# Moving weight sums, head transposes, convolution passes and the next part's input inside a hand-ordered decoder-layer kernel

## The reference, cut to what matters

```
u = rmsnorm(x) @ w_in                         # 1024 -> q, k, v, gates, o, B, C, h
h = sigmoid(o) * HeadRMSNorm(mLSTM(q, k, v, gates))       # 4 heads, chunkwise with running state
y = B * causal_depthwise_conv3(C * h_conv)                # 3 taps, 512 channels
x = x + concat(h, y) @ w_out
x = x + (silu(f @ w_gate) * (f @ w_up)) @ w_down          # f = rmsnorm(x), D_FF = 2816
x = x + sigmoid(x @ w_pg) * rmsnorm(p @ w_ple)
y = rmsnorm(x)
```

## Time and profile before

| | |
|---|---|
| median of three runs | 2736.15 us |
| the profiled execution's own time | 2736.39 us |
| its span, first to last instruction | 2734.7 us |
| TensorE busy (matmul) | 2522.9 us, 92% |
| VectorE, ScalarE, GpSimd busy | 54%, 35%, 42% |
| mean granted TensorE clock | 0.966 of full |
| DMA | 456.46 MB, 167 GB/s on average |
| weight conversions, ScalarE and GpSimd | 696 each |
| sums stored in part 0, loaded later | 168 stores, 336 loads of 512 KB |

### The profile page before, as it was taken

How to read it: one execution, slowest core, us unless ns; L and a number is a source line. 1 busy time by engine, 2 the same in 40 slices (tenths; PEclk the granted TensorE clock), 3 DMA queues, 4 the chain that set the end, 5 groups by cost and what they waited for, 6 DMA issues and landing times.

```text
span 2734.7 us, 41185 instructions
## 1 busy us (share of the span) xinstructions
PE 2522.9 (92%) x15882; PEld 2458.5 (90%) x15882; DVE 1479.8 (54%) x2288; ACT 952.8 (35%) x1766; POOL 1138.3 (42%) x939
## 2 busy tenths in 40 slices
PE   4999788999999779999999999998998999999998
PEld 4889787999999778899999999997888989999997
DVE  5656787765546664447753333466455674333355
ACT  4344443333333534334422222253223442222233
POOL 3556655665555443333332333333422333233333
PEclk6999899999999989999999999998999999999998
DMA  5435534554444646456455545474545645554544
GB/s 163 168 139 199 178 116 147 177 188 160 169 168 149 201 141 198 141 182 202 154 178 166 152 149 162 150 232 151 178 141 178 198 159 175 186 163 153 161 142 161
DMA packets 306309, 456.46 MB, mean 167 GB/s; under 512 B 21683, under 2 KB 218596, under 8 KB 305606
## 3 DMA queue, kind: packets, MB, share of 16 engines
q1 hardware_dynamic: 239014, 269.13, 29.8%
q10 hardware_dynamic: 67104, 184.70, 21.4%
HBM read 347.44 MB, written 106.35 MB: 166 GB/s over the span
## 4 chain that ended last, share of the span: by engine, by line
PE 47%; DVE 4%; issue 2%; DMA 2%; ACT 1%; POOL 1%; DVEq 0%; POOLq 0%; SPq 0%; ACTq 0%
PE bank L503 15%; PE bank L504 15%; PE bank L505 15%; DMA wring<-weight_parts 1%; DVE ess L2130 0%; POOL wring L2400 0%; DVE qlo L1553 0%; PE bank L602 0%; PE bank L665 0%; PE bank L613 0%; DMA xs<-x_prompt 0%; PE bank L668 0%; DVE R L1712 0%; PE bank L671 0%; DMA wraw<-w_out 0%
## 5 line engine op out<-in xcount | busy, mean ns | idle before, releaser
L2400 POOL TENSOR_TENSOR wring<-wraw,wring 128x512 fp32r<-128x512 f32 x612 | 875.8, 1437 | 1309.2 <-ACT wring L1118 1305.2
L503 PE MATMUL bank<-qhi,wring 128*128 128x352 f32 (+1 forms) x3588 | 1183.6, 330 | 132.9 <-issue 31.2
L505 PE MATMUL bank<-qhi,wring 128*128 128x352 f32 (+1 forms) x3588 | 1165.8, 325 | 0.0
L504 PE MATMUL bank<-qlo,wring 128*128 128x352 f32 (+1 forms) x3588 | 1165.1, 325 | 0.0
L503 PEld LDWEIGHTS bank<-qhi,wring 128*128 128x128 f32 x3588 | 691.9, 193 | 157.4 <-issue 149.1
L504 PEld LDWEIGHTS bank<-qlo,wring 128*128 128x128 f32 x3588 | 691.9, 193 | 0.0
L505 PEld LDWEIGHTS bank<-qhi,wring 128*128 128x128 f32 x3588 | 688.5, 192 | 0.0
L1118 ACT ACTIVATE wring<-wraw 128x512 fp32r<-128x512 f32 x612 | 382.2, 628 | 867.3 <-PE bank L505 735.1
L503 PE MATMUL bank<-hid,wring 128*128 128x352 f32 (+1 forms) x1056 | 341.2, 323 | 14.5 <-DVE wide L2217 7.5
L505 PE MATMUL bank<-hid,wring 128*128 128x352 f32 (+1 forms) x1056 | 339.6, 322 | 0.0
L504 PE MATMUL bank<-hid,wring 128*128 128x352 f32 (+1 forms) x1056 | 338.9, 321 | 0.0
(11 more groups left out here) (302 smaller groups left out, 2429.2 us busy)
## 6 DMA issues: line engine op xcount, KB each, us to landing
wring<-weight_parts ACTq DMA_DIRECT2D x336, 512.0 KB, 4.1
weight_parts<-wring SPq DMA_DIRECT2D x168, 512.0 KB, 3.1
wraw<-w_down SPq DMA_DIRECT2D x33, 1024.0 KB, 6.5
wraw<-w_in SPq DMA_DIRECT2D x27, 512.0 KB, 4.6
wraw<-w_in SPq DMA_DIRECT2D x12, 1024.0 KB, 6.3
wraw<-w_gate SPq DMA_DIRECT2D x11, 1024.0 KB, 5.8
wraw<-w_up SPq DMA_DIRECT2D x11, 1024.0 KB, 5.8
wraw<-w_gate SPq DMA_DIRECT2D x22, 512.0 KB, 4.2
```

What stands on the lines that cost most here:

```text
L503: nc.tensor.matmul(o, hi, mh, start=begins, stop=False, skip_group_check=True)
L504: nc.tensor.matmul(o, hi, ml, start=False, stop=False, skip_group_check=True)
L505: return nc.tensor.matmul(o, lo, mh, start=False, stop=ends, skip_group_check=True)
L2400: nc.gpsimd.tensor_tensor(wlo[e % RING][:, :].rearrange(v, k=k), w.src, whi[e % RING][:, :].rearrange(v, k=k), ALU.subtract).then_inc(lo_d ...
```

## The change

1. Spare sums. The 16 sums of the four pg pairs of part 0 are no longer made in pg but in part 0's feed-forward, two in each of gate and up pairs 3, 5, 7, 9, behind the third and the sixth entry of the pair. For each, VectorE makes the sum in place in a new buffer `spare_raw`, ScalarE and GpSimd convert it into a ring slot that no product reads, and SyncE stores it. Four loads of 1 MB fill `spare_raw` (SyncE, at raw numbers 24, 30, 36, 42; the first waits for the spread of the embedding's roots). Pg of part 0 then loads its sums as parts 1 and 2 do.
2. Heads. The transposes move from m = 8c+8 to 8c+10, in part 2's last chunk to 8c+9 (with its offset of 11, m = 52), its sample chunk from 8 to 11. ScalarE's exponentials wait for a semaphore of its own earlier squares.
3. Convolution. Each channel group's three passes are spread over three steps, m = 14 to 19 and 42 to 47.
4. Next x. Tiles 0 and 1 are loaded when the last hidden halves are made, not after the last down product; their squares move into the last down block. Transposes go behind products 2, 4, ..., 12, roots to step 13, spread behind 15, normalising from step 16, the low halves to steps 22, 24, 25, 26 (operand 5 among them). T4 and the low halves of 6 and 3 go in front of the last `gated_add`.

```diff
+SPARE_PAIRS = (3, 5, 7, 9) if SPARE else ()
+SPARE_SUMS = ("S1", "S3", "S2", "S4")
...
-            for kind, m in (("scores", 1), ("outputs", 4), ("transposes", 8)):
+            last = self.sample and c == self.nch - 1
+            for kind, m in (("scores", 1), ("outputs", 4), ("transposes", 9 if last else 10)):
...
         for j, n in enumerate(names):
...
+            if j in (2, 5) and spares:
+                add_spare(made[0][0], spares[j // 3])
...
+            def spare_weights(i):
+                if i:
+                    sp.wait_ge(lo_done, spare_last[i - 1])
+                else:
+                    sp.wait_ge(*written[("e", 0)])
+                sp.dma_start(spare_raw[...], w_pg_v[:, :, 256 * i:256 * i + 256]).then_inc(spare_in, 16)
...
-                    act.wait_ge(prod, entry_end[e - RING])
+                    if entries[e - RING].spare is None:
+                        act.wait_ge(prod, entry_end[e - RING])
...
+            def ahead():
+                one_ahead()
+                if n_hi[0] < len(entries) and entries[n_hi[0]].spare is not None:
+                    one_ahead()
...
-                    if m in (14, 16, 42, 44):
-                        convolve(q, m // 42, (m % 28 - 14) // 2)
+                    if m >= 0 and m % 28 in range(14, 20):
+                        convolve(q, m // 28, (m % 28 - 14) // 3, (m % 28 - 14) % 3)
...
-                        if 5 <= s <= 15 and s % 2:
+                        if 2 <= s <= 12 and s % 2 == 0:
...
-                    for at_, part in ((19, "B11"), (20, "T1"), (21, "B21"), (22, "B22"), (23, "T2"), (24, "T3")):
+                    for at_, part in ((16, "B11"), (17, "T1"), (18, "B21"), (19, "B22"), (20, "T2"), (23, "T3")):
-                    if s in (23, 25, 27):
-                        low_of(nxt, "in", {23: 0, 25: 4, 27: 1}[s])
+                    if s in (22, 24, 25, 26):
+                        low_of(nxt, "in", {22: 0, 24: 4, 25: 1, 26: 5}[s])
...
-                gated_add(q, 3, 1)
-                gated_add(q, 3, 0)
                 if q.n < 2:
                     nxt = supers[q.n + 1]
                     in_part(nxt, "T4")
-                    for i in (5, 6, 3):
+                    for i in (6, 3):
                         low_of(nxt, "in", i)
+                gated_add(q, 3, 1)
+                gated_add(q, 3, 0)
```

More of the change, by code:

```diff
@@ L307, in add_pairs @@
                 made.append((r, views, turn[m]))
-                where = {n: e0 + len(members) * j + m for j, n in enumerate(names)}
+                shift = [sum(1 for k in range(len(spares)) if 3 * k + 2 < j) for j in range(len(members) * len(names))]
+                where = {n: e0 + len(members) * j + m + shift[len(members) * j + m] for j, n in enumerate(names)}
                 for j, n in zip((0, 4, 6, 10) if two else (0, 1, 3, 6), turns):
-                    sums_at.setdefault(e0 + j + m, []).append((n, r, at_, where, turn[m], first, second))
-        for n in names:
-            for r, views, turn_ in made:
+                    sums_at.setdefault(e0 + j + m + shift[j + m], []).append((n, r, at_, where, turn[m], first, second))
+        for j, n in enumerate(names):
+            for m, (r, views, turn_) in enumerate(made):
                 if n in views:
@@ L535, in product @@
                 n_entry[0] += 1
+                if n_entry[0] < len(entries) and entries[n_entry[0]].spare is not None:
+                    n_entry[0] += 1
             def pair(q, st, i, after, base):
@@ L1073, in _ @@
                         keep_parts((now - 1,))
+                    if q.n < 2 and r == 52:
+                        next_tiles(supers[q.n + 1], (2, 3))
             gains(3)
@@ L1094, in link, with one_ahead @@
                 act.wait_ge(act_own, n_own[0])
-            def ahead():
+            def one_ahead():
                 e = n_hi[0]
@@ L1489, in _ @@
                         high_of(q, "pg", 4)
+                    if q.n < 2 and e in (3, 4):
+                        next_squares(supers[q.n + 1], e - 3)
                 high_of(q, "pg", 1)
@@ L1523, in copy_at, with spare_sum, one_ahead @@
                 return nc.vector.tensor_scalar(out, in_, 1.0, None, mul)
-            def ahead():
+            def spare_sum(n):
+                i, m, v = n // 4, n % 4, by_quarters(spare_raw)
+                name = SPARE_SUMS[m]
+                if m == 0:
+                    dve.wait_ge(spare_in, 16 * (i + 1))
+                else:
+                    dve.wait_ge(spare_sums, n)
+                out, a, b, op = {"S1": ("A22", "A21", "A22", add), "S3": ("A21", "A11", "A21", sub),
+                                 "S2": ("A11", "A22", "A11", sub), "S4": ("A12", "A12", "A11", sub)}[name]
+                nc.vector.tensor_tensor(v[out], v[a], v[b], op).then_inc(spare_sums, 1)
+            def one_ahead():
                 e = n_sum[0]
                 n_sum[0] += 1
+                if e < len(entries) and entries[e].spare is not None:
+                    spare_sum(entries[e].spare)
                 for name, r, v, where, turn, first, second in sums_at.get(e, ()):
@@ L1549, in ahead @@
                         nc.vector.tensor_tensor(v["A11"], v["A12"], second[:, :, :], sub).then_inc(sums, 1)
+            def ahead():
+                one_ahead()
+                if n_sum[0] < len(entries) and entries[n_sum[0]].spare is not None:
+                    one_ahead()
             def low_of(q, st, i):
@@ L2401, in ahead @@
                                         ALU.subtract).then_inc(lo_done, 1)
+            def ahead():
+                one_ahead()
+                if n_lo[0] < len(entries) and entries[n_lo[0]].spare is not None:
+                    one_ahead()
             def low_of(q, st):
```

131 lines of the change are left out of this document (80 added, 51 removed).

## The result

The changed kernel takes 2706.36 us (median; 2705.51 to 2709.41) against 2739.2 us for the kernel before on the same chip: 0.9883 of its time, 95% interval 0.986 to 0.9906. That is 1.2% or 32.8 us less, clear of the noise; 36.3 us less (2700 us) were forecast. The profiled execution took 2705.51 us, its span is 2703.8.

The account below looks back on a forecast made before the run. TensorE, busy 92% of the span, was taken as the bound, so only its waits or clock falls could be won. Terms -8.9 - 27.9 - 7.0 - 11.0 + 5.5 + 13 = -36.3 from 2736.4 gave 2700 us; range 2682 to 2723.

Parts of the forecast that it names:

- Pg of part 1: Last down product to product 2 of the next `in`: moved x steps cut 85.3 to 76.4 us, -8.9.
- Pg of part 0: Same stretch in part 0: spare sums leave and x steps move, 105.9 to 78.0 us, -27.9.
- Rivals 2 and 4: 2: next x comes no earlier, 2711 us, chance 0.16; 4: part 0's pg keeps its waits, 2719 us, 0.05.
- Feed-forward of part 0: Added spare sums and halves delay VectorE at gate pairs: +13 us together, bounds +3 and +28.
- clock: Part 0's feed-forward: waits of about 2.5 to 3 us are near where the clock fell; 2 us.
- The shared port: VectorE sums and GpSimd low halves lock each other out; by that rule the gate-pair term is 14 us, not 8.
- Heads: Ten head transposes' waits of 7.0 us all go, -7.0; bounds 4 and 8.
- convolution: Waits for VectorE's eviction of P6 shrink by 7.5 us, plus clock and a late eviction: -11.0, bounds 6 and 13.
- last heads of part 2: Eviction queued behind a `w_out` entry delays VectorE's merge: +4.0 us, +1.5 for the clock; bounds 2 and 6.
- Part 2's merge: VectorE's merge must wait until 2117.3, +4.0 us; part 2's first `out` product then waits 8 to 9 us.
- Rival 1: Ring exposed: TensorE waits a whole entry at each of 16 spares, with clock falls, 69 us; total 2756, chance 0.06.
- Rival 3: Feed-forward pays back over half part 0's pg gain through VectorE and GpSimd locking at every spare: 2715 us, chance 0.13.

Follow-up runs that it names:

- experiments 1 and 2: Experiment 1 has its own line; experiment 2 is the changed kernel run again unaltered, as a yardstick: 2703.58 us.
- experiment 6: Changed kernel with the next x's moves undone (loads, transposes, low halves, gated-add order), spare sums kept: 2713.69 us.
- Experiment 1: Changed kernel without the spare sums; part 0's pg makes its own sums again, everything else stays moved: 2700.58 us.
- experiment 3: Changed kernel with the 16 spare sums on VectorE left out, their loads, conversions and stores kept (wrong sums): 2688.0 us.
- experiment 4: Changed kernel with the 16 spare entries in part 0's down blocks 1 to 4 instead of gate and up pairs: 2680.36 us, 2679.69 repeated.
- experiment 5: Changed kernel with one spare entry a pair from up 3 to gate 9, two each in up 9 and gate 10: 2696.62 us.

## Why the prediction was right, point by point

The mechanism of the two pg stages came out as forecast, in size too. That the total is off by only 3.5 us (5.4 by the spans) is in part luck: the price in the feed-forward was put too low, and errors in the split of the other terms cancelled. The spare sums, the main part of the change, were to gain about 6 us on balance and gained nothing in the totals of experiments 1 and 2.

- **Pg of part 1**: -8.9 forecast, -9.1 measured, -9.0 by experiment 6. The end stands at 76.2 (76.4 forecast), product 27 waits 4.0 us (about 5).
- **Pg of part 0**: -27.9 forecast, -28.8 measured; 77.1 against 78.0. Experiment 1 parts it into 20.6 for the sums and 8.2 for the moves. Rivals 2 and 4 are out.
- **Feed-forward of part 0**: this is the term that was too small, 13 forecast and 20.4 measured by the windows, 19.4 between the same instructions. By its own steps: the four waits at gate pairs 3, 5, 7 and 9 are 3.22, 2.84, 3.29 and 3.34 against 0.81, 0.52, 0.59 and 0.52, so +10.3 (8 forecast); those at 4, 6, 8 and 10 are about 1.5 against 0.6, so +3.6 (2); the first spare load, 0 (1: the wait at gate pair 2 is 1.56 in both). The size that was off most is the **clock**, 2 forecast: from gate pair 2 to gate pair 10 TensorE took 344.4 us before and 365.9 after, 21.5 more, of which 13.8 are longer waits and 7.7 slower running, with no instruction added. The prediction judged the clock by one wait of 4.00 after which it fell and one of 2.80 after which it did not the earlier trace rows, and took 2 us for waits of 2.5 to 3, though its own sum put such a wait at each of four gate pairs. It fell after all four. About 2 us came back where the prediction had no term: at the end of the last down block TensorE waited 0.89 and 1.09 us for VectorE, which makes a sum for pg there, in before and in experiment 1, and not where pg's sums are made early.
- **The shared port.** The spare sum at 522.11 began 0.42 us into a low half and ended 0.55 us after it, where a sum alone takes 0.68. The Trainium skill, page "SBUF — State Buffer", section "Who interferes with whom", would have each such operation wait for the other to end; this row agrees. By that rule the waits at the four gate pairs were to grow by 14 us, by my 2.0 a pair by 8; they grew by 10.3. Six of the eight sums took 1.76 to 1.79 us, the first ones of gate pairs 7 and 9 took 0.68. The sums make 6.4 of the 10.3 (12.7 with them, 6.3 without in experiment 3); the rest goes with the conversions, loads, stores and ring places.
- **Heads, convolution, last heads of part 2**: -7.0, -11.0 and +5.5 make -12.5; the stretches outside pg and part 0's feed-forward show -15.0 (-1.7, -5.7, -7.6; -14.0 with the start at its -0.7), and +1.6 in a feed-forward that was not changed. The sum is near, its split was wrong. The head waits are gone as foretold, but undoing that edit costs under 2 us; the convolution is worth 21 once the heads are late. Its remaining waits are 1.96 in part 0 (1.4 forecast), 1.40 in part 1 (the first row below) and none in part 2, as forecast. The near sum is luck.
- **Part 2's merge** is late by the mechanism named, but not by 4.0: the entry of `w_out` landed and was converted at 2081.25, the heads were evicted at 2081.79, and the merge started 2.8 us later, counted from the eviction of P5, than in before. T1 then ran in 1.56 instead of 2.51 us. So the wait is 6.14, not 8 to 9.

```profile
1115.17 0.40 PE L533 MATMUL bank<-qhi,wring 128*128 128x352 f32 x1 [1.40 <-DVE u L1683]
...
2081.25 0.63 ACT L1164 ACTIVATE wring<-wraw 128x512 fp32r<-128x512 f32 x1 [3.88 <-DMA wraw<-w_out]
2081.79 1.12 ACT L1290 ACTIVATE wide<-bank,gmh 128x128 f32<-128x128 f32 x4
...
2090.67 0.62 PE L533 MATMUL bank<-qhi,wring 128*128 128x336 f32 x1 [6.14 <-DVE qlo L1630]
```

- **Rival 1** (ring exposed) did not come: no wait for a `wring` entry in that feed-forward. Rival 3 had the right place and half of the 15 us that it added.
- **Readings that were wrong**: the clock line of the earlier trace rows has no weak pair in the thirteenth to fifteenth slices. It has a 6 in the first and an 8 in the fifth, fifteenth, twenty-eighth and last; only the fifteenth lies at part 0's pg. The windows of rows 2 carry that argument alone. And GpSimd does more than low halves of weights: it makes operands' low halves too.

In all: 36.3 forecast less 7.4 for the feed-forward and 1.6 for part 1's, plus 1.1 in pg and 2.5 in the rest, is the 30.9 us of the spans.

## What to carry to other kernels

Work moved into a stage "with slack" must be placed by the queue of the engine that does it: the same 16 entries cost 18 us in gate and up pairs, where VectorE frees the banks just in time, and nothing in the down blocks, where it has room (in experiment 4 it is busy for 11.4 of the first block's 30.7 us). Price a stall with the clock that it costs: here waits that grew by 14 us in all, 10 of them at four places, took nearly 8 us more with the clock. And two edits that fill the same engine's queue can be one term; undo each alone, and both together, before crediting either. Both together was not run here.

## What the runs showed of the hardware

The clock fell after shorter waits than rows 9 had led me to think: after 2.84, 3.22, 3.29 and 3.34 us (changed kernel), and three times after 1.89 us (experiment 5), once not after 1.90, and never after the waits of 1.40 to 1.67 us of the stretch in experiment 3, though they are 13.7 us in all. It need not fall at once: the wait of 2.84 us ended at 616.23, and the instructions went to 0.29 us apart only at 617.43 (granted clock 0.99 until 617.4, 0.50 from there to 620.6).

```profile
616.23 0.40 PE L533 MATMUL bank<-qhi,wring 128*128 128x352 f32 x1 [2.84 <-DVE u L1683]
...
617.43 0.50 PE L534 MATMUL bank<-qlo,wring 128*128 128x352 f32 x1
617.72 0.50 PE L535 MATMUL bank<-qhi,wring 128*128 128x352 f32 x1
```
